# Moving value rows of an expert mixer from TensorE to VectorE in every second pair

## What is computed

```
s = einsum('thpc,hpkc->thpk', q, sub_keys)             # two sides of 128 keys, 8 heads
top, pos = top_k(s1[..., None] + s2[..., None, :], 16) # idx: 16 of 16384 experts a head
g = softmax(top)
a = gelu(einsum('thkd,td->thk', u_tab[idx], x))        # u rows of 1024
w = g * a
out = einsum('thk,thkd->td', w, v_tab[idx])            # v rows of 1024, summed over 8 x 16
```

## Time and profile before

| | |
|---|---|
| median of 3 runs | 4381.66 us (4379.17 to 4395.21) |
| the profiled execution | 4382.4 us, of it 4380.7 from the first to the last instruction |
| mean granted TensorE clock | 0.881 |
| TensorE busy | 3387.2 us, 77% |
| VectorE busy | 2805.3 us, 64% |
| ScalarE busy | 1581.6 us, 36% |
| GpSimd busy | 1218.1 us, 28% |
| moved by DMA | 1471.58 MB, mean 336 GB/s |

### The profile page before, as it was taken

The page is one execution under the profiler, slowest core; times in us unless marked ns, Lnnn a source line. Parts: engine busy times, 40 slices in busy tenths (PEclk is TensorE's granted clock), DMA queues, the critical chain, the costliest instruction groups (busy, mean ns, idle before and its releaser), DMA issues.

```text
span 4380.7 us, 33898 instructions
## 1 busy us (share of the span) xinstructions
PE 3387.2 (77%) x10219; PEld 1760.2 (40%) x10219; DVE 2805.3 (64%) x6049; ACT 1581.6 (36%) x3679; POOL 1218.1 (28%) x1122
## 2 busy tenths in 40 slices
PE   5785867985987778989599678567978777777766
PEld 2572445842434445544144344224533222222221
DVE  0213365557657785646877788676867777667687
ACT  1212154422226563432222465344433233333333
POOL 0001111213222222323333232242323344444433
PEclk9897978997997789999799778768999889999999
DMA  4767856889986787879999798888989999999998
GB/s 174 266 236 277 327 188 235 318 335 400 346 336 228 275 305 305 344 295 371 405 394 418 299 338 299 287 333 344 414 340 382 395 415 421 414 421 413 404 371 370
DMA packets 277901, 1471.58 MB, mean 336 GB/s; under 512 B 40581, under 2 KB 91781, under 8 KB 127125
## 3 DMA queue, kind: packets, MB, share of 16 engines
q0 software_dynamic: 156672, 1140.92, 65.7%
q1 hardware_dynamic: 121044, 328.49, 20.5%
HBM read 1408.90 MB, written 60.40 MB: 335 GB/s over the span
## 4 chain that ended last, share of the span: by engine, by line
PE 41%; DMA 25%; DVE 18%; issue 7%; ACT 6%; POOL 2%; SPq 1%; POOLq 0%; DVEq 0%; ACTq 0%
DMA c_ring<-in_uv,l_idx 17%; PE c_p_y L1154 11%; DVE c_ring L1670 7%; PE c_PB L850 4%; PE c_PC L850 4%; DVE l_ysb L1686 3%; PE c_PA L1107 3%; PE c_PA L1062 2%; PE c_PB L1062 2%; PE c_PC L1062 2%; PE c_PB L1107 2%; POOL c_ring L1784 2%; PE c_PA L1090 1%; PE c_PC L1065 1%; PE c_PB L1065 1%
## 5 line engine op out<-in xcount | busy, mean ns | idle before, releaser
L1784 POOL DMA_INDIRECT c_ring<-in_uv,l_idx x1088 | 1211.2, 1113 | 3139.1 <-PE c_p_y L1154 1341.4
L1154 PE MATMUL c_p_y<-c_ring,l_diag 128*128 128x512 f32 (+1 forms) x2816 | 1515.6, 678 | 443.3 <-ACT l_diag L1325 433.0
L1670 DVE CUSTOM_DVE_ANT_0 c_ring<-c_ring,l_h_cur 128x1024 f32<-128x1024 f32 x1088 | 1302.8, 1221 | 369.3 <-DMA c_ring<-in_uv,l_idx 360.7
L1154 PEld LDWEIGHTS c_p_y<-c_ring,l_diag 128*128 128x128 f32 (+1 forms) x2816 | 552.9, 207 | 1233.0 <-ACT l_diag L1325 643.6
L1317 ACT ACTIVATE l_gel<-l_dots 128x2 f32<-128x2 f32 x544 | 110.7, 203 | 1607.2 <-DVE l_dots L1670 1606.0
L1686 DVE SCALAR_TENSOR_TENSOR l_ysb<-c_ring,l_wgt,l_ysb 128x1024 f32<-128x1024 f32 x384 | 492.5, 1282 | 0.0
L1317 ACT ACT_TABLE_LOAD x207 | 265.6, 1283 | 59.8 <-DVE l_dots L1670 56.5
L1320 ACT ACTIVATE l_wgt<-l_gel,l_gw 128x1 f32<-128x1 f32 x1088 | 261.2, 287 | 17.9
L1325 ACT ACTIVATE l_diag<-c_ident,l_wgt 128x128 f32<-128x128 f32 x640 | 243.0, 399 | 16.7
L850 PE MATMUL c_PB<-c_area 128*128 128x451 f32 (+1 forms) x576 | 226.3, 545 | 0.0
L850 PE MATMUL c_PC<-c_area 128*128 128x451 f32 (+1 forms) x576 | 224.4, 541 | 0.1
(11 more groups left out here) (275 smaller groups left out, 3676.9 us busy)
## 6 DMA issues: line engine op xcount, KB each, us to landing
c_area<-in_w_gb SPq DMA_DIRECT2D x32, 2304.0 KB, 9.5
c_area<-in_w_in SPq DMA_DIRECT2D x32, 1804.0 KB, 9.4
c_area<-rw_sp SPq DMA_DIRECT2D x16, 2048.0 KB, 10.5
c_ring<-in_uv,l_idx POOLq DMA_INDIRECT x1088, 10.1
c_area<-in_w_out SPq DMA_DIRECT2D x8, 2048.0 KB, 9.7
proj<-c_area SPq DMA_DIRECT2D x64, 225.5 KB, 7.2
c_area<-proj SPq DMA_DIRECT2D x8, 1288.0 KB, 6.6
c_area<-in_x_all SPq DMA_DIRECT2D x16, 512.0 KB, 18.8
```

The lines of the kernel that those rows point to most:

```text
L1154: ins = mm_(p_y[:T, e * 512:(e + 1) * 512], diag[:, j, :T], ring[:, j, D + e * 512:D + (e + 1) * 512], start=r == 0 and q == 0 and k == 0, ...
L1670: ins = nc.vector.tensor_tensor_reduce(out=ring[:, j, 0:D], in0=ring[:, j, 0:D], in1=h_cur[i % 2][:, :], scale=1.0, scalar=0.0, op0=ALU.mu ...
L1784: nc.gpsimd.indirect_dma_start(out=ring[:, j, :], out_offset=None, in_=t_in["uv"][:, :], in_offset=bass.IndirectOffsetOnAxis(ap=idx[:, hea ...
```

## The change

Which rows VectorE adds is no longer decided by the tile alone, but by the plan. In a pair of tiles 0 to 5 with odd q that has an `in_unit`, `gate`, `out` or `sco` step beside it, VectorE adds both rows, TensorE none, and ScalarE makes no diagonal matrix. All other pairs stay as they were. GpSimd's waits count accordingly, and `s_vdone` counts only the pairs in which TensorE sums something.

The plan has 83 pairs of the new kind: 18 beside tile 0, 31 beside tiles 1 and 2, 34 beside tiles 3 to 5. Placed in the stretches of the run, from the first to the last front step of a kind:

| stretch, us | beside | pairs | of the new kind |
|---|---|---|---|
| 412 to 535 | in_unit | 11 | 5 |
| 535 to 730 | the last in_unit, mixers | 13 | 1 |
| 730 to 880 | gate | 14 | 7 |
| 880 to 925 | out | 3 | 1 |
| 925 to 994 | out, sco | 8 | 4 |
| 994 to 1106 | nothing, in_prep | 17 | 0 |
| 1106 to 1290 | in_unit | 23 | 11 |
| 1290 to 1664 | mixers | 36 | 0 |
| 1664 to 1882 | gate | 28 | 11 |
| 1882 to 1982 | out | 10 | 3 |
| 1982 to 2088 | sco | 13 | 6 |
| 2088 to 2200 | nothing, in_prep | 19 | 0 |
| 2200 to 2422 | in_unit | 36 | 12 |
| 2422 to 2984 | mixers | 68 | 0 |
| 2984 to 3220 | gate | 37 | 11 |
| 3220 to 3330 | out | 12 | 3 |
| 3330 to 3458 | sco | 21 | 8 |
| 3458 to 3540 | nothing | 15 | 0 |
| 3540 to 4381 | nothing (last group) | 160 | 0 |

```diff
-def apart(n):
-    return ALL_PAIRS[n][0] < GROUPS[-1][0]
...
+PLAN = make_plan()
+
+def rows_apart():
+    rows = []
+    for expert, beside in PLAN:
+        if expert and expert[0] == "pair":
+            _, i, r, q = expert
+            long = any(step[0] in ("in_unit", "gate", "out", "sco") for step in beside)
+            two = long and q % 2 == 1
+            rows.append(() if i >= GROUPS[-1][0] else (0, 1) if two else (1,))
+    return rows
+
+APART = rows_apart()
+APART_BEFORE = [sum(len(x) for x in APART[:n]) for n in range(len(APART) + 1)]
+SUMMED_BEFORE = [sum(len(x) < PAIR for x in APART[:n]) for n in range(len(APART) + 1)]
...
+            rows_here = [k for k in range(PAIR) if k not in apart(n)]
+            if not rows_here:
+                return
             pe.wait_ge(s_diag, n + 1)
-            for k in range(1 if apart(n) else PAIR):
+            for k in rows_here:
...
-            ins.then_inc(s_ae, 1)
-            act.wait_ge(s_ae, n_e + 2)
-            for k in range(1 if apart(n) else PAIR):
-                ins = nc.scalar.mul(diag[:, (n * PAIR + k) % RING, :T], unit[:, :T], wgt[:, c0 + k:c0 + k + 1])
+            rows_here = [k for k in range(PAIR) if k not in apart(n)]
+            if rows_here:
+                n_weigh[0] += 1
+                ins.then_inc(s_ae, 1)
+                act.wait_ge(s_ae, n_weigh[0])
+                for k in rows_here:
+                    ins = nc.scalar.mul(diag[:, (n * PAIR + k) % RING, :T], unit[:, :T], wgt[:, c0 + k:c0 + k + 1])
             ins.then_inc(s_diag, 1)
...
+            for m_, k in enumerate(apart(n)):
+                j, col, done = (n * PAIR + k) % RING, q * PAIR + k, apart_before(n) + m_
                 dve.wait_ge(s_xres, 16 * (i + 1))
-            if n:
-                dve.wait_ge(s_vapart, apart_before(n))
-            dve.wait_ge(s_diag, n + 1)
-            y = ysb[i % 2]
-            nc.vector.scalar_tensor_tensor(out=y[:T, :], in0=ring[:T, j, D:2 * D], scalar=wgt[:T, col:col + 1],
-                                           in1=y[:T, :], op0=ALU.mult, op1=ALU.add).then_inc(s_vapart, 1)
+                if done:
+                    dve.wait_ge(s_vapart, done)
+                dve.wait_ge(s_diag, n + 1)
+                nc.vector.scalar_tensor_tensor(out=y[:T, :], in0=ring[:T, j, D:2 * D], scalar=wgt[:T, col:col + 1],
+                                               in1=y[:T, :], op0=ALU.mult, op1=ALU.add).then_inc(s_vapart, 1)
...
             if n >= RING // PAIR:
-                pool.wait_ge(s_vdone, n - RING // PAIR + 1)
+                if summed_before(n - RING // PAIR + 1):
+                    pool.wait_ge(s_vdone, summed_before(n - RING // PAIR + 1))
                 if apart(n - RING // PAIR):
                     pool.wait_ge(s_vapart, apart_before(n - RING // PAIR + 1))
```

More of the change, by code:

```diff
@@ L81, in pair_index @@
     return (i * HEADS + r) * 8 + q if i < TILES else TILES * HEADS * 8 + r * 4 + q
-def apart(n):
-    return ALL_PAIRS[n][0] < GROUPS[-1][0]
-def apart_before(n):
-    return sum(apart(k) for k in range(n))
 ALL_PAIRS = [(i, r, q) for i in range(NT) for r in range(HEADS) for q in range(pairs_of(i))]
@@ L180, in make_plan, with apart, apart_before, summed_before @@
     return plan
+PLAN = make_plan()
[11 more added lines that the diff above has]
+SUMMED_BEFORE = [sum(len(x) < PAIR for x in APART[:n]) for n in range(len(APART) + 1)]
+def apart(n):
+    return APART[n]
+def apart_before(n):
+    return APART_BEFORE[n]
+def summed_before(n):
+    return SUMMED_BEFORE[n]
 class Scope:
@@ L263, in layer @@
     sb, pb, sem = m.sb, m.pb, m.sem
-    PLAN = make_plan()
     wa2, ba_bc, go_bc, bf_bc, gq_bc, gk_bc, gm_bc = c.wa2, c.ba_bc, c.go_bc, c.bf_bc, c.gq_bc, c.gk_bc, c.gm_bc
@@ L1164, in _ @@
     def _(act):
-        n_chain = [0]
+        n_chain, n_weigh = [0], [0]
         def link(ins):
@@ L1315, in weigh @@
             act.wait_ge(s_dot, n + 1)
-            n_e = 2 * n
+            n_weigh[0] += 1
             a_(gel[:, c0:c0 + PAIR], dots[:, c0:c0 + PAIR], ACT.Gelu).then_inc(s_ae, 1)
-            act.wait_ge(s_ae, n_e + 1)
+            act.wait_ge(s_ae, n_weigh[0])
             for k in range(PAIR):
@@ L1675, in values @@
         def values(n):
-            if n < 0 or not apart(n):
+            if n < 0:
                 return
             i, r, q = ALL_PAIRS[n]
-            T, j, col = width_of(i), (n * PAIR + 1) % RING, q * PAIR + 1
-            if r == 0 and q == 0:
+            T, y = width_of(i), ysb[i % 2]
+            for m_, k in enumerate(apart(n)):
+                j, col, done = (n * PAIR + k) % RING, q * PAIR + k, apart_before(n) + m_
                 dve.wait_ge(s_xres, 16 * (i + 1))
-            if n:
-                dve.wait_ge(s_vapart, apart_before(n))
-            dve.wait_ge(s_diag, n + 1)
-            y = ysb[i % 2]
-            nc.vector.scalar_tensor_tensor(out=y[:T, :], in0=ring[:T, j, D:2 * D], scalar=wgt[:T, col:col + 1],
-                                           in1=y[:T, :], op0=ALU.mult, op1=ALU.add).then_inc(s_vapart, 1)
+                if done:
[3 more added lines that the diff above has]
+                                               in1=y[:T, :], op0=ALU.mult, op1=ALU.add).then_inc(s_vapart, 1)
         def finish(i):
@@ L1691, in finish @@
             r, q = HEADS - 1, pairs_of(i) - 1
-            dve.wait_ge(s_vdone, pair_index(i, r, q) + 1)
+            dve.wait_ge(s_vdone, summed_before(pair_index(i, r, q) + 1))
             dve.wait_ge(s_xres, 16 * (i + 1))
```

## The result

The changed kernel took 4326.27 us (median of 4 runs, 4324.80 to 4338.17) against 4388.43 for the kernel before (4 runs, 4379.17 to 4398.01): a ratio of 0.9863 [0.9844, 0.9882]. That is faster by 60 to 62 us, inside the range and in the direction forecast, 24 us above the forecast of 4302. The profiled execution took 4327.66 us with a span of 4325.9, so between the two profiles 54.8 us were gained where 79.8 were forecast. The question of this study is where the other 25 went.

A forecast was written before the change was run, and what follows sets the result against it. Each stretch was taken to have its own limit: TensorE, DMA engines, or chains. Gains per stretch, 1.72 us a row where TensorE limits, summed to 79.8 us, giving 4302 us; forecast 4275 to 4327 (0.58), wider range 4268 to 4369 (0.82).

The forecast's parts named there:

- The price of a row: Stretches that TensorE fills: each value row taken off TensorE was claimed to gain 1.72 us.
- the forecast had taken something off for full transfers: Stretch 925 to 994: four pairs, 6.9 us in full, 4.1 by the DMA share; 5.5 was forecast.
- VectorE's rows are hidden: VectorE's 83 added rows, 108 us, lie beside TensorE's or DMA's work: priced at nothing, 1.3 us a pair if uncovered.
- took the middle, 16: in_unit, 1106 to 1290: eleven pairs, gain 12.9 us if share 1.00 is the wall, 18.9 if 412 GB/s is.
- The rival that rested on a lower wall: Mixed loads and stores as in 1106 to 1290 can't exceed 357 GB/s: gain 39.7 us, time 4342; chance 0.05.
- The change touches none of their pairs: Mixers (1290 to 1664) and pairs with nothing beside them (2088 to 2200), bound by chains or DMA: no gain claimed.
- earlier or at the same time: GpSimd's gathers in 1106 to 1290, which waited 108.8 us for TensorE's row: ring slots released no later than before.
- the one at 1902.28: out, 1882 to 1982: this pair has 4.86 us of TensorE idle behind it, waiting for weights; gain nothing.
- Half of each: DMA-full stretches 2984 to 3220 and 3330 to 3458: up to 7.1 and 2.6 us possible, 3.5 and 1.3 taken.
- the `out` row there: Stretch 3220 to 3330: one of its three pairs was taken to gain 1.7 us.
- The rival needed 0.76: Clock rival, long DMA-full stretches: TensorE pauses more; at clock 0.69, 70 us slower, 4452; decides from 0.76 down; chance 0.09.

## Why the prediction was right, and where its sum failed

The terms against the two profiles (times of the kernel before name the part, cut at the first and last step of a kind; between two parts nothing was gained or lost; gains in us, a minus is a loss):

| part | forecast | measured |
|---|---|---|
| `in_unit`, 412 to 535 | 8.6 | 8.6 |
| `gate`, 730 to 880 | 12.0 | 10.8 |
| `out` and `sco`, 880 to 1106 | 7.2 | 7.0 |
| `in_unit`, 1106 to 1290 | 16 | 18.8 |
| mixers, 1290 to 1654 | 0 | -8.4 |
| `gate`, 1654 to 1885 | 18.9 | 19.0 |
| `out`, 1895 to 1960 | 3.4 | -2.9 |
| `sco`, 1984 to 2080 | 7.2 | 8.6 |
| all from 2203 to 3449 | 6.5 | 0 |
| before 412, 535 to 730, after 3449 | 0 | -6.7 |
| sum | 79.8 | 54.8 |

**Right.** The price of a row is 1.72 us where TensorE fills a stretch at its upper clock: six parts agree within 3 us each. One of them, `out` and `sco` from 880 to 1106, agrees only as a sum, and in part by luck: its stretches gave 2.6, 0.7 and 3.7 us for a forecast of 1.7, 5.5 and 0. Two of the four rows of 925 to 994 stand at its edges and show in the stretches beside it. For the other two the forecast had taken something off for full transfers, but the share was 0.94 before and 0.93 after, and what took the gain away was the clock, 2.8 us (below). VectorE's rows are hidden but for 3 to 11 of their 106 us, and the two experiments that take them away or keep them alone show it (0.9857 and 1.0025). TensorE didn't wait for VectorE in the two longest filled stretches: the one at 1084 and that at 1632 are 100% busy. The DMA-full stretch keeps its length (225.9 for 222) at a share of 0.99.

**Sized by the wrong wall.** The prediction couldn't tell whether a share of 1.00 or a rate of 412 GB/s is the wall and took the middle, 16. The full 18.9 was there: the share went to 1.00, the rate from 357 to 396. With the share as the wall the stretch could not have been under 171.1; it is 165.2. The Trainium skill, "DMA: Bandwidth & Descriptors", section "Where 436 GB/s comes from", puts the HBM side of a core at about 358 GB/s; the trace doesn't agree, with 394 to 405 GB/s in five of the stretches above. The rival that rested on a lower wall falls with it.

**"The change touches none of their pairs", and a release "earlier or at the same time": the failed step.** The mixers were priced at nothing because they lose no row, and of the three `out` rows of 1895 to 1960 two at 1.7 each and the one at 1902.28 at nothing, for the 4.86 us of idle time behind it. The two were about right (2 to 3 us together for 3.4). But a pair that leaves TensorE out frees its slot when VectorE is done, and the prediction took earlier as something that can only help. At two places earlier means two gathers beside a load that TensorE waits for: 5 us at `hT`, and at the weights of `out` 6 us in the changed kernel and 2 to 4 in the three others with the same rows. Each wait is as before in the kernels that give that one pair its row back. That is 7 to 11 of the 25 us, at two pairs of 83. The other 3 us of the mixers are not settled: over the kernels that keep the first pair's row and don't add rows ahead of them this part takes 366.7 to 376.7 us, 370.4 before.

**Halves in DMA-full stretches.** "Half of each" of a possible 9.7 us and the `out` row there were worth 0 together, and the 34 late pairs alone gave 1.0013. A share of 0.97 was a full one.

**The rest.** The first `in_unit` beside tile 0 begins at 414 to 424 us over all kernels, though none of them moves a row ahead of it. 3.0 us there, 1.6 from 535 to 730 and 2.1 in the last group, 6.7 together, are no larger than such differences between kernels that are alike at that place; whether the change has a part in them is open.

**The clock.** In the three late stretches it is 0.94 to 0.96 of the upper level (2.4 GHz), 0.97 to 0.99 before: taking rows out does make TensorE pause more, and it changes no length there by more than 4 us. The rival needed 0.76. In the stretch of 925 to 994, though, the clock took a row's gain away. Before, the row of the pair (0, 5, 1) stood between a wait and the first `sco` step:

```profile
925.43 3.58 PE L1154 MATMUL c_p_y<-c_ring,l_diag 128*128 128x512 f32 x4 [1.50 <-ACT l_diag L1325]
928.85 7.03 PE L1107 MATMUL c_PA<-c_area 128*128 128x512 f32 x16
```

After the change the step itself follows a wait:

```profile
911.29 9.83 PE L1131 MATMUL c_PA<-c_area 128*128 128x512 f32 x16 [2.06 <-ACT c_area L1310]
```

The row ran at a granted clock of 0.53, close to the lower level (1.2 GHz), and the step behind it at 1.00; without the row the step runs at 0.72 and takes 2.8 us longer (9.66 us to the next start, times 0.72, is the 7.0 of before). The same step takes 9.3 to 10.0 us in the five kernels that leave this row out and 7.0 to 7.6 in four that keep it; in the other three two steps run on end.

## What to carry to other kernels

Price a row moved off an engine stretch by stretch: full where that engine is busy for 100% at its upper clock, nothing where transfers or weights end the waits, and not half in between. A row right behind a wait may run at the lower clock, and then the next step can inherit that clock when the row goes. When a buffer comes free earlier, look at what its next transfer will run beside: a load that the path waits for gets slower, though it is in another queue, and one pair left as it was can be worth more than its row (5 us of the wait for `hT` against 1.72). Once a stretch's transfers are full, more relief for the engine only moves the wait to the next step that needs a transfer, so put the remaining rows beside the steps with transfers to spare.

## What was not expected of the hardware

A DMA share of 0.93 was no proof that 7% was left: the same stretch went from 357 to 396 GB/s (11%) while the share rose from 0.93 to 1.00 (7.5%). Two more gathers issued beside it made a load of 1536 KB land 24.7 us after its issue instead of 19.1, and two that went out 3 us sooner made one of 2048 KB land in 21.6 instead of 16.5. And a VectorE row that waits for the one before, in the same buffer, starts with 0.09 us of idle time.
